# Attention's eight heads written out on TensorE, and the latent projections' side work moved between engines and slots

## The reference

```python
h = rmsnorm(x, g_pre);  proj = h @ w_in      # split into c_q 768, c_kv 256, k_pe 32, gates, hq, hf, hi, merge logits
q  = (rmsnorm(c_q, g_q) @ w_uq)              # 8 heads x (64 plain + 32 rotary)
kv = (rmsnorm(c_kv, g_kv) @ w_ukv)           # 8 heads x (64 keys + 64 values); rotary key k_pe shared by all heads
attn = chunk_causal_attention(q, k, v)       # softmax over all keys of chunks (64 rows) up to the query's own
y_a = (attn * silu(gate_a)) @ w_branch_a
y_b = (rmsnorm(hgrn2(hq, hf, hi)) * silu(gate_b)) @ w_branch_b
m = sigmoid(..) * y_a + sigmoid(..) * y_b;   x = x + rmsnorm(m @ w_out, g_post)
```

## Time and profile before

| | us |
|---|---|
| median of 3 runs | 2385.24 (2384.97 to 2397.46) |
| profiled execution | 2389.71, of which its span 2387.9 |
| PE busy | 2218.7 (93%) |
| DVE busy | 1029.5 (43%) |
| ACT busy | 907.4 (38%) |
| POOL busy | 352.4 (15%) |
| latent projections, from the last product before them to attention's first row of its own | about 1201 to 1450 |
| attention's eight heads | about 1450 to 2000 |

### The profile page before, as it was taken

The page is one execution under the profiler, slowest core; times in us unless marked ns, Lnnn a source line. Parts: engine busy times, 40 slices in busy tenths (PEclk is TensorE's granted clock), DMA queues, the critical chain, the costliest instruction groups (busy, mean ns, idle before and its releaser), DMA issues. The chain is left out here.

```text
span 2387.9 us, 33689 instructions
## 1 busy us (share of the span) xinstructions
PE 2218.7 (93%) x11664; PEld 1841.0 (77%) x11664; DVE 1029.5 (43%) x1824; ACT 907.4 (38%) x1683; POOL 352.4 (15%) x240
## 2 busy tenths in 40 slices
PE   6999999999979999999956998989999998899998
PEld 5888888778768888888845777778787786788886
DVE  6000000000014445445446546767777776665652
ACT  7111111000114444444335234656666565443441
POOL 1222224022101111111112220000000013200000
PEclk9999999999989999999977999999999999999999
DMA  5222222221312333233166564331133326663751
GB/s 182 84 65 76 74 74 74 84 101 62 105 48 76 97 97 97 92 97 95 63 228 209 165 195 109 69 71 39 44 65 71 69 60 190 196 208 124 222 153 67
DMA packets 213202, 256.51 MB, mean 107 GB/s; under 512 B 39360, under 2 KB 138048, under 8 KB 209600
## 3 DMA queue, kind: packets, MB, share of 16 engines
q1 hardware_dynamic: 188352, 208.21, 30.6%
q10 hardware_dynamic: 23616, 43.00, 4.8%
q0 software_dynamic: 1152, 4.19, 0.5%
HBM read 157.31 MB, written 98.04 MB: 107 GB/s over the span
## 5 line engine op out<-in xcount | busy, mean ns | idle before, releaser
L74 PE MATMUL bankD<-hT_hi,shared_w_hi 128*128 128x512 f32 x512 | 212.4, 415 | 11.7 <-POOLq L703 11.7
L74 PE MATMUL bankA<-hT_hi,shared_w_hi 128*128 128x512 f32 x544 | 212.5, 391 | 0.0
L75 PE MATMUL bankA<-hT_lo,shared_w_hi 128*128 128x512 f32 x544 | 211.8, 389 | 0.0
L76 PE MATMUL bankA<-hT_hi,shared_w_lo 128*128 128x512 f32 x544 | 211.7, 389 | 0.0
L76 PE MATMUL bankD<-hT_hi,shared_w_lo 128*128 128x512 f32 x512 | 202.0, 394 | 0.0
L75 PE MATMUL bankD<-hT_lo,shared_w_hi 128*128 128x512 f32 x512 | 201.0, 393 | 0.0
L1766 DVE TENSOR_REDUCE small_chunk_min<-scores 128x1 f32<-128x512 f32 (+2 forms) x320 | 181.1, 605 | 44.0 <-PE scores L76 29.6
L1786 ACT ACTIVATE probs<-scores,small_least 128x1024 f32<-128x1024 f32 (+2 forms) x192 | 167.4, 872 | 11.8 <-DVE small_least L1773 10.6
L74 PE MATMUL bankA<-wt_hi,hT_hi 128*128 128x512 f32 x384 | 152.6, 397 | 12.7 <-DVE shared_v_raw L392 7.7
L313 ACT ACTIVATE stage<-bankA 128x512 f32<-128x512 f32 x68 | 40.7, 598 | 301.6 <-PE bankA L76 300.1
L74 PE MATMUL scores<-k_sb,q_sb 96*128 96x512 f32 (+2 forms) x320 | 127.6, 399 | 25.5 <-ACT probs L1786 15.7
(11 more groups left out here) (247 smaller groups left out, 4715.9 us busy)
## 6 DMA issues: line engine op xcount, KB each, us to landing
projT<-stage ACTq DMA_DIRECT2D x68, 256.0 KB, 2.4
shared_w_raw<-in_w_in_dram SPq DMA_DIRECT2D x32, 512.0 KB, 4.3
projT<-d_stage ACTq DMA_DIRECT2D x64, 256.0 KB, 2.4
e_l_in<-projT SPq DMA_DIRECT2D x64, 256.0 KB, 4.8
gateTok<-stage ACTq DMA_DIRECT2D x32, 256.0 KB, 2.0
shared_w_lo<-hgTok SPq DMA_DIRECT2D x16, 512.0 KB, 3.4
knT<-b_out SPq DMA_DIRECT2D x32, 256.0 KB, 2.8
vTok<-b_out SPq DMA_DIRECT2D x32, 256.0 KB, 2.9
```

The source lines that it names most:

```text
L74: pe.matmul(out, a_hi, b_hi, start=first, stop=False)
L75: pe.matmul(out, a_hi, b_lo, start=False, stop=False)
L76: return pe.matmul(out, a_lo, b_hi, start=False, stop=last)
```

## The change

There are three parts.

1. On PE the loop over the three pairs of heads is gone: all four pairs are written out. The instructions of a head are the same.
2. The remainders of the 40 turned tiles move from POOL to DVE. DVE makes that of tile i - 1 right after it has scaled tile i; that of the last key tile comes before the first value split, that of the last plain query tile before the rotation, and those of the two rotary tiles one slot after the rotation, behind that slot's jobs. POOL now only waits for the last sum before it goes on to its part of the next stage.
3. The side work is spread otherwise. The last weights, two at each of (KV, 2, 4) to (KV, 2, 6) before, now are two at (KV, 2, 4) and one at each of (KV, 3, 0) to (KV, 3, 3). The six pieces of the second query block, one at each of (KV, 3, 1) to (KV, 3, 6) before, are now beside the first query block (2, 2, 1, 1). Sums and spreads of the KV blocks stand one tile later; the sum of Q 1 stands at the end of block Q 0 and no longer at the end of KV 3; the spread of Q 0 stands after the first tile of KV 3 and no longer after the last of KV 2. The roots and reciprocals move with them.

```diff
--- before.py
+++ after.py
@@ -1162,10 +1162,13 @@
             beside(KV, 2, i, ("c", Q, 0, 4 + i))
         beside(KV, 2, 2, ("c", KV, 3, 0))
         beside(KV, 2, 3, ("c", KV, 3, 1))
-        for i in range(3):
-            beside(KV, 2, 4 + i, ("w", 12 + 2 * i), ("w", 13 + 2 * i))
-        for i in range(KQ):
-            beside(KV, 3, 1 + i, ("c", Q, 1, i))
+        beside(KV, 2, 4, ("w", 12), ("w", 13))
+        for i in range(4):
+            beside(KV, 3, i, ("w", 14 + i))
+        beside(Q, 0, 0, ("c", Q, 1, 0), ("c", Q, 1, 1))
+        beside(Q, 0, 1, ("c", Q, 1, 2), ("c", Q, 1, 3))
+        for i in range(2):
+            beside(Q, 0, 2 + i, ("c", Q, 1, 4 + i))
         for blk in (1, 2):
             beside(Q, blk, 0, ("c", Q, blk + 1, 0), ("c", Q, blk + 1, 1))
             for i in range(4):
@@ -1282,16 +1285,7 @@
         def gpsimd(pool):
             pool.memset(eps[:], EPS).then_inc(const_set, 1)
             pool.memset(ones[:], 1.0).then_inc(const_set, 1)
-
-            def split_out(g, blk, i):
-                e, use = number(g, blk, i), turn_use(g, blk, i)
-                pool.wait_ge(out_hi, use + 1)
-                pool.tensor_tensor(out[:, e % OUTS, 1], turned[:, use % TURNED], out[:, e % OUTS, 0].bitcast(F32), ALU.subtract)\
-                    .then_inc(out_lo, 1)
-
-            for g, blk in BLOCKS:
-                for i in range(V_AT if g == KV else Q_EV):
-                    split_out(g, blk, i)
+            pool.wait_ge(sums_done, len(NORMS))
 
         def scalar(act, attend):
             act.wait_ge(const_set, 2)
@@ -1363,6 +1357,8 @@
                 round_weights(m)
             root(KV, 0)
             for g, blk in BLOCKS:
+                if (g, blk) == (KV, NB - 1):
+                    take_spread(Q, 0)
                 if g == KV or blk > 0:
                     take_spread(g, blk)
                 for i in range(EVICTIONS[g]):
@@ -1378,15 +1374,11 @@
                         attend.first_exponentials(act, row)
                     if (g, blk, i) == (KV, 2, 5):
                         root(Q, 0)
-                    if (g, blk, i) == (KV, 2, 7):
-                        take_spread(Q, 0)
                     if g == Q and blk == 0 and i in (1, 3):
                         round_shared_key(i // 2)
                 if g == KV and blk + 1 < NB:
                     root(KV, blk + 1)
-                if (g, blk) == (KV, NB - 1):
-                    root(Q, 1)
-                if g == Q and 0 < blk < NB - 1:
+                if g == Q and blk < NB - 1:
                     root(Q, blk + 1)
 
         def vector(dve, attend):
@@ -1439,6 +1431,12 @@
                 o = out[:, e % OUTS].rearrange("p a (h c n) -> p (a h) c n", c=2, n=VD)
                 dve.scalar_tensor_tensor(o[:, :, 1], per_head(bank[:, bank_of(e)], VD), rstd[:, KV, t:t + 1],
                                          o[:, :, 0].bitcast(F32), ALU.mult, ALU.subtract).then_inc(v_lo, 1)
+
+            def split_out(g, blk, i):
+                e, use = number(g, blk, i), turn_use(g, blk, i)
+                dve.wait_ge(out_hi, use + 1)
+                dve.tensor_tensor(out[:, e % OUTS, 1], turned[:, use % TURNED], out[:, e % OUTS, 0].bitcast(F32), ALU.subtract)\
+                   .then_inc(out_lo, 1)
 
             def rotate(blk):
 
@@ -1483,14 +1481,22 @@
             for g, blk in BLOCKS:
                 for i in range(EVICTIONS[g]):
                     if g == KV and i >= V_AT:
+                        if i == V_AT:
+                            split_out(KV, blk, V_AT - 1)
                         split_value(blk, i)
                     elif i < X_AT:
                         scale(g, blk, i)
+                        if i > 0:
+                            split_out(g, blk, i - 1)
                     for row in ROWS_BESIDE.get((g, blk, i), ()):
                         attend.first_minima(dve, row)
                     if g == Q and i == X_AT:
+                        split_out(Q, blk, X_AT - 1)
                         scaled_table(blk)
                         rotate(blk)
+                    if g == Q and i == X_AT + 1:
+                        split_out(Q, blk, X_AT)
+                        split_out(Q, blk, X_AT + 1)
                     for job in BESIDE.get((g, blk, i), ()):
                         if job[0] == "c":
                             prepare(*job[1:])
@@ -1504,9 +1510,7 @@
                     split_shared_key(1)
                 if g == KV and blk + 1 < NB:
                     inverse(KV, blk + 1)
-                if (g, blk) == (KV, NB - 1):
-                    inverse(Q, 1)
-                if g == Q and 0 < blk < NB - 1:
+                if g == Q and blk < NB - 1:
                     inverse(Q, blk + 1)
 
         def tensor(pe, attend):
@@ -1544,9 +1548,9 @@
                 else:
                     pe.wait_ge(cross_ready, blk * 4 + 2 * (i - X_AT + 1))
 
-            SUMS_AFTER = {(KV, 0, 1): (KV, 0), (KV, 0, 6): (KV, 1), (KV, 1, 6): (KV, 2), (KV, 2, 4): (Q, 0), (KV, 2, 6): (KV, 3),
-                          (KV, 3, 7): (Q, 1), (Q, 1, 5): (Q, 2), (Q, 2, 5): (Q, 3)}
-            SPREAD_AFTER = {(KV, 0, 3): (KV, 0), (KV, 1, 1): (KV, 1), (KV, 2, 1): (KV, 2), (KV, 2, 7): (Q, 0), (KV, 3, 1): (KV, 3),
+            SUMS_AFTER = {(KV, 0, 1): (KV, 0), (KV, 0, 7): (KV, 1), (KV, 1, 7): (KV, 2), (KV, 2, 5): (Q, 0), (KV, 2, 7): (KV, 3),
+                          (Q, 0, 5): (Q, 1), (Q, 1, 5): (Q, 2), (Q, 2, 5): (Q, 3)}
+            SPREAD_AFTER = {(KV, 0, 3): (KV, 0), (KV, 1, 2): (KV, 1), (KV, 2, 2): (KV, 2), (KV, 3, 0): (Q, 0), (KV, 3, 2): (KV, 3),
                             (Q, 1, 0): (Q, 1), (Q, 2, 0): (Q, 2), (Q, 3, 0): (Q, 3)}
 
             for g, blk in BLOCKS:
@@ -2032,11 +2036,9 @@
                         output.tensor_beside(pe, step)
 
             pe.wait_ge(first_v, 16)
-            with pe.Fori(0, PAIRS - 1) as pair:
+            for pair in range(PAIRS):
                 for u in range(2):
-                    head(pair, u, True)
-            for u in range(2):
-                head(PAIRS - 1, u, u == 0)
+                    head(pair, u, pair < PAIRS - 1 or u == 0)
 
     return sems, Attend(sync=sync, masks=masks, scalar=scalar, vector=vector, tensor=tensor,
                         load_first_keys=load_first_keys, load_first_shared_key=load_first_shared_key,
```

## The result

In five runs each, the changed kernel took 2371.84 us (2369.61 to 2375.12) and the kernel before 2396.87 (2384.97 to 2398.36). The ratio is 0.9922, with a 95% interval of 0.9899 to 0.9945: 18.6 us faster, 13 to 24. (The two medians differ by more, 25.0, because the five runs of the kernel before fall into two groups, two near 2385 and three near 2397; the ratio is the figure to go by.) A later comparison, six runs against eleven, gave the same, 0.9922 (0.9898 to 0.9946). The forecast was faster by 23.8, a ratio of 0.990, near the good end of both intervals. The forecast time of 2361.5 was 10.3 too low. By the ratio, about 5 of these are the gain and 5 the base: the base was the median of three runs, 2385.24, which are three of the five above, and 32 later runs of the kernel before had a median of 2390.15, from 2385.29 to 2400.48.

The account below looks back on a forecast made before the run. PE bounds the kernel, losing time at stops for late DVE and ACT, at head borders, and at its lower clock. Projections 10.0 + 2.2 = 12.2 plus attention 11.6 give 23.8 us off 2385.24: 2361.5, range 2352 to 2375.

Parts of the forecast that it names:

- The 0.7 saved in a slot: KV 2 slots with side work: without POOL's remainder DVE's addition ends sooner, so a slot takes 3.2 us instead of 3.86.
- the cover: KV 2 slots: DVE's new remainder, about 0.6 us, fits in the 1.28 us DVE waits for ACT, so costs nothing.
- The waits of ACT for key stores: Value slots: ACT waits for SP's key stores before rounding; priced only in KV 1, appearing there named as a sign of error.
- The stop before the spread of Q 1: End of block Q 0: PE may stop 2.0 us, bounds 0 and 4, because DVE's slots there carry more.
- the 2.2 us of the last Q blocks: Without POOL, 0.7 us saved before the sum of Q 2 and 1.5 in block Q 2; bounds 0.7 and 3.
- rival B: Attention gains 11.6 us, projections only about 4, as DVE or SP's stores become late; total 15.6, 2369.5 us; chance 0.18.
- Three borders: PE in attention, heads 1 to 2, 3 to 4, 5 to 6: 14.22, 13.47, 9.42 us become 8.5 each, 11.6 saved.
- 7.7 to 8.9 at all of them: Expected profile sign: every border of heads takes 7.7 to 8.9 us from fold to first value product on PE.
- C: Writing out heads gains nothing, the 4.58 us stop not being the jump's; only the projections' 12.2 come, 2373 us; chance 0.08.
- E: Slower: the written-out program is fetched too late at every border of heads, 5.35 us each; 2399 us; chance 0.04.
- D: Gains in both projections and attention shrink, to 2 to 5 us in all; 2382 us; chance 0.05.
- F: More than the sum: PE keeps full clock in KV blocks, Q 1's spread waits for nothing; 2356 us; chance 0.05.

## Where the prediction was right, and which of its steps failed

**The stages.** Projections 12.2 forecast, 12.1 measured on the average of the traces; attention 11.6 and 10.9. The mechanisms were read rightly: waits of PE, then the slot that makes them, then the border of heads. Two things failed: a term of the sum in the projections, whose 12.2 came out by two errors that cancel, and the base. From mark 1, in us, in the two traces of before and the four of the changed kernel; "earlier by" is the difference of the means:

| | before | changed | earlier by | forecast |
|---|---|---|---|---|
| first scale of KV 3 | 96.19, 96.72 | 92.84, 91.71, 89.97, 93.09 | 4.6 | 2.9 |
| first Q product | 115.21, 115.73 | 101.76, 100.63, 98.90, 102.02 | 14.6 | 13.0 |
| spread of Q 1 | 146.01, 146.11 | 135.13, 134.01, 131.99, 135.39 | 11.9 | 10.0 |
| end of the stage | 252.2, 251.9 | 241.0, 240.1, 237.6, 241.1 | 12.1 | 12.2 |

**Part 2 in the KV blocks.** The first scale of KV 3 came 3.4 earlier in the first traces and 4.6 on average, more than the forecast's upper bound of 4.3. The 0.7 saved in a slot is 0.68, and the cover is as wide as it was read: a second 0.6 us operation goes in free. The waits of ACT for key stores, priced at nothing outside KV 1 because a slot of `out` has 12 us and a store lands in 2.9, did come in the other blocks too (1.98 the longest, in KV 2 of the first trace). That reading was wrong, though what it cost does not show.

**Part 3.** From KV 3's first scale to the first Q product it took 8.92 or 8.93 us in all four traces, 8.9 forecast. The stop before the spread of Q 1 was forecast at 2.0 and is 1.97 to 2.00, and the sum takes 0.95 at the full clock, 1.05 forecast.

**The step that failed: the 2.2 us of the last Q blocks.** Each of the two stops did shrink as worked out, 4.73 to 4.07 and 5.47 (5.41 in the second trace) to 4.07, 2.1 in all. The stage kept 0.2 of it: 11.9 at the spread of Q 1, 12.1 at its end. What the term put at nothing is the clock behind the stops: from that spread to the end of the stage, 16 or 18 products of 512 columns ran at the lower level in the traces of before, and 27 to 30 in those of the changed kernel. Eleven more, at 0.2 us each (0.427 less 0.227), are, by estimate, 2.2 us. They are not all behind the new stop of 1.97: one of the four traces has that stop and no slow product from there to the sum of Q 2 (25.67 us, where the others took 27.25 to 27.29 and the kernel before 26.22), and more of them later. Why more products run slow after smaller stops stays open. That the total of 12.2 was met all the same, because 1.9 more came ahead of that spread than forecast, is luck.

**A second thing that the sum had right by luck.** It added part 2 and part 3. By one trace each, part 3 without part 2 is worth 0.8 us in the stage, not 7: with the remainders on POOL the Q blocks lose what was won ahead of them. Part 2 without part 3 is worth 4.8 and both are worth 11.2. The rival B named the place (Q 1's spread), but no rival had the two hang on each other.

**Part 1.** Three borders were taken to fall to 8.5 each, 11.6 less in all. On the average of the traces they took 38.3 together before and 26.2 after, 12.1 less, while the four borders that the change doesn't touch went from 32.9 to 33.8: 11.1 in all. So the term was near on average and off in a single execution: in the first trace the three are 7.66, 8.64 and 11.24, 9.6 less than in the first of before. The sign "7.7 to 8.9 at all of them" failed: over four traces of the changed kernel the 28 borders run from 7.64 to 11.24.

**What the whole measured, and the base.** The two stages sum to 23.0 in the traces and the timed ratio says 18.6 with 24 as its bound. Whether 1 to 2 us go lost in the output stage, or the timed runs fell as they did by scatter, these runs don't settle. The forecast time failed by a second step: 2385.24 was too low a base by about 5 us, and the profiled execution at 2389.71 and the run at 2397.46, both at hand, had said that three runs do not fix it. Of the rivals, C is out by the kernel with one jump, E because no written-out border in any trace has a stop of over 1.3 us, D by the stages, F by the stop of 1.97. B's total of 15.6 lies within the timed interval; it is out by the stage, which gained 12.1 and not 4.

## What to carry to other kernels

A small operation on a third engine isn't free because that engine is idle: here it made 15 of DVE's 24 additions, with both inputs in SBUF, wait for it, 0.7 us each, and moving it to the busier engine shortened the stage by 4.8 us in the old order of the side work and by 10.4 in the new one. Look for the pause that the busier engine has anyway before giving work away. Edits to the order of side work and to its owners should be priced together and also each without the other. When stops shrink, don't count on all of it: count the products at the lower clock behind them too. And take the base from more than three runs when the kernel's own scatter (15 us) is as large as the gain.

## What the runs showed of the hardware that was not expected

The same instructions, with the same pause of 1.25 us at a head's border, take 7.65, 8.6 to 9.7 or 11.2 us from fold to value product. What differs is TensorE's clock: at 7.65 nothing in between runs at its lower level, at 11.2 all twelve of the score products of 512 columns do (duration 0.63 instead of 0.39), and in between up to seven of them or the short products and transposes around them (at a border of 8.64, four transposes took 1.07 instead of 0.62). One execution had 9.1 at six of its seven borders, others one of 11.2 and most of the rest at 7.7. Nothing that TensorE did ahead of a border, as far as I looked, tells the cases apart, so the cause is open. It is worth 1 to 3.6 us a border, and is much of why attention took anything from 536.3 to 547.9 us in the ten traces without a jump.

A jump back in PE's program cost 4.88 to 6.61 us from fold to scores in the seven that were recorded, against 1.25 straight on and 1.52 to 1.68 on leaving a loop.
